# A gated-linear-attention stage in another order: TensorE turns tiles two ahead and across heads, GpSimd takes products and the normalising

## The reference

```python
log_a = log_sigmoid(lr @ w_a2 + b_a) / 16      # decay, 128 per head and token
b = cumsum(log_a)                              # within a chunk
q_t, k_t = q * 128 ** -0.5 * exp(b), k * exp(-b)
k_e = k * exp(b_last - b)
p = tril(q_t @ k_t.T)
o = p @ v + q_t @ S                            # S: state entering the chunk
S = exp(b_last) * S + k_e.T @ v
o = rmsnorm(o, g_head) * silu(g)               # then w_out
```

## Time and profile before

| | us |
|---|---|
| median of 3 runs | 3666.15 (3665.55 to 3667.69) |
| the profiled execution, its own time | 3667.28 |
| its span | 3665.7 |
| mean granted clock of TensorE | 0.953 |
| GLA, from the first state product (647.80) to the next stage's first load (1013.74) | 365.9 |

### The profile page before, as it was taken

One profiled execution on the slowest core, in us unless ns is written; L12 is line 12 of the kernel. 1 busy time (PEld: TensorE's weight loads), 2 busy tenths in 40 slices (PEclk: granted clock), 3 DMA queues, 4 the chain that ended last, 5 costly groups with the idle time before them and its releaser, 6 DMA issues. The chain is left out here.

```text
span 3665.7 us, 50108 instructions
## 1 busy us (share of the span) xinstructions
PE 3333.9 (91%) x17844; PEld 2414.2 (66%) x17844; DVE 1675.5 (46%) x2027; ACT 1398.8 (38%) x2277; POOL 718.8 (20%) x775
## 2 busy tenths in 40 slices
PE   7999997877779799999999799999999996888798
PEld 6999997433368699999999344444444443444387
DVE  5111121766633321111121589788888884333333
ACT  5111111545421111111111578777877783223321
POOL 0000000000001000000000466566666662000000
PEclk9999998888889899999999799999999998999899
DMA  4222122333254432222221623323232204999843
GB/s 140 70 69 69 64 65 77 110 115 117 77 185 165 142 116 69 69 71 74 74 64 54 179 80 95 90 64 93 81 109 53 58 18 138 368 365 372 324 146 105
DMA packets 240030, 439.34 MB, mean 120 GB/s; under 512 B 24821, under 2 KB 148538, under 8 KB 227802
## 3 DMA queue, kind: packets, MB, share of 16 engines
q1 hardware_dynamic: 224714, 351.87, 28.9%
q0 software_dynamic: 15152, 85.34, 6.5%
HBM read 313.03 MB, written 124.13 MB: 119 GB/s over the span
## 5 line engine op out<-in xcount | busy, mean ns | idle before, releaser
L1623 POOL TENSOR_TENSOR att_w<-att_w,att_rest 128x1023 f32<-128x1023 f32 (+7 forms) x384 | 613.1, 1599 | 375.5 <-DVE att_rest L1588 372.5
L451 PE MATMUL projb_acc<-projb_x_hi,projb_w_hi 128*128 128x416 f32 x1280 | 452.9, 354 | 26.5 <-DVE projb_x_lo L441 26.5
L451 PE MATMUL projb_acc<-projb_x_hi,projb_w_lo 128*128 128x416 f32 x1280 | 450.6, 352 | 0.0
L451 PE MATMUL projb_acc<-projb_x_lo,projb_w_hi 128*128 128x416 f32 x1280 | 450.3, 352 | 0.0
L1495 PE MATMUL att_z<-att_k,att_q 64*128 64x512 f32 (+3 forms) x1280 | 402.7, 588 | 2.7 <-ACT att_w L1546 2.7
L1538 ACT ACTIVATE att_rest<-att_z,att_bias 128x1024 f32<-128x1024 f32 (+7 forms) x384 | 332.8, 867 | 135.3 <-PE att_z L1495 113.7
L1459 PEld LDWEIGHTS att_wT_acc<-const_ident,att_w 128*128 128x128 f32 x2176 | 232.7, 141 | 216.5 <-issue 116.2
L1588 DVE TENSOR_TENSOR_SCAN att_rest<-att_rest,att_zero 128x128 f32<-128x128 f32 (+7 forms) x256 | 358.5, 1405 | 21.9 <-ACT att_rest L1538 21.1
L288 PE MATMUL proja_acc<-proja_x_hi,proja_w_hi 128*128 128x416 f32 x1000 | 353.5, 353 | 0.8 <-DVE proja_x_lo L261 0.7
L288 PE MATMUL proja_acc<-proja_x_hi,proja_w_lo 128*128 128x416 f32 x1000 | 351.4, 351 | 0.0
L288 PE MATMUL proja_acc<-proja_x_lo,proja_w_hi 128*128 128x416 f32 x1000 | 349.7, 350 | 0.0
(11 more groups left out here) (220 smaller groups left out, 4597.3 us busy)
## 6 DMA issues: line engine op xcount, KB each, us to landing
smp_k_pages<-in_cache_k SPq DMA_DIRECT2D x128, 512.0 KB, 9.2
smp_v_pages<-in_cache_v SPq DMA_DIRECT2D x128, 512.0 KB, 10.0
proj_b<-projb_out POOLq DMA_DIRECT2D x32, 1040.0 KB, 4.7
proj_a<-proja_out POOLq DMA_DIRECT2D x24, 1040.0 KB, 4.5
att_q<-proj_b SPq DMA_DIRECT2D x64, 256.0 KB, 4.0
att_k<-proj_b SPq DMA_DIRECT2D x14, 1024.0 KB, 12.8
proja_w_raw<-in_w_in_a SPq DMA_DIRECT2D x24, 512.0 KB, 4.1
gla_vgT<-proj_a SPq DMA_DIRECT2D x24, 512.0 KB, 6.1
```

The source lines that it names most:

```text
L451: mm = pe.matmul(acc[:, q, 0:size], w[:, b, k, :], x[:, k, at:at + size], start=(k == 0 and w is w_hi and x is x_hi), stop=(k == KD - 1 an ...
L1623: pool.tensor_tensor(these, these, passed[:, 1:size], ALU.mult).then_inc(w_made, 1)
```

## The change

`normalise_project` multiplies the gate by the head's gain `g_head` as well (`gate_gains`, one small load more), so that GLA needs no gain. In `gla`:

- TensorE turns tile t + 2 before it makes tile t's products across chunks and tile t + 1's products within. The list runs over the end of a head: tiles 0 and 1 of the next head are turned, and tile 0's inner products made, around the sample tile. Tile 0 has no product with a state, and the first chunk's state is copied, not cleared and updated; `S` is a ring of eight, and only the eighth chunk of a head waits until the old state is stored.
- GpSimd, which had nothing to do in GLA's loop, makes `gap`, the three products of a span, and the norm: one product with `rstd` broadcast over the span, one with the gate. It does so one span after the other, the last one of a head after the sample tile. The norm of span u is in the list at tile 4u + 5.
- The inverse root is exp(-0.5 ln(mean)) on ScalarE, in the table that exp and ln use already, and one Newton step of four small instructions on VectorE (`refine`). The factor 128 ** -0.5 goes into the exp as a bias.
- `logit`, `work`, `b_sum`, `gap` have two buffers; the steps are numbered 0 to 8.
- The eight sample state products use three buffers, and three of them come before the products with `s_in`.

The core of the diff:

```diff
+                    dve.scalar_tensor_tensor(out=out[:, b, at:at + size], in0=out[:, b, at:at + size],
+                                             scalar=gate_gains[:, b:b + 1], in1=acc[:, q, 0:size], op0=ALU.mult,
+                                             op1=ALU.mult).then_inc(gate_made, 1)
...
+        STEPS = (((7, 1), (8, 1)), ((0, 2), (1, 2), (2, 2), (3, 2)), ((4, 2),), ((5, 2), (6, 2)))
...
+        for t in range(NT):
+            order += [("turn", (t + 2) // n_tiles, (t + 2) % n_tiles), ("across", 0, t)]
+            order += [("root", 0, t // 4)] if t % 4 == 3 and t < NT - 1 else []
+            if t + 1 < NT:
+                order.append(("within", 0, t + 1))
+            order += [("normalise", 0, t // 4 - 1)] if t % 4 == 1 and t > 4 else []
+            for k, n in STEPS[t % 4]:
+                order.append(("prep", (t // 4 + n) // NCH, (t // 4 + n) % NCH, k))
+        order += [("sample", 0), ("root", 0, NCH - 1), ("turn", 1, 1), ("normalise", 0, NCH - 1), ("within", 1, 0)]
+        first = [("prep", 1, 0, k) for k in range(9)] + [("prep", 1, 1, k) for k in range(7)]
+        first += [("turn", 1, 0), ("turn", 1, 1), ("within", 1, 0)]
...
+                        pe.wait_ge(in_v[u], h * 16 + (16 * off + 16))
+                        pe.wait_ge(in_g[u], h * 16 + (16 * off + 16))
+                    pe.wait_ge(tok_cp, earlier + ONE)
...
+                    if t % 4 == 0 and t < NT:
+                        pe.wait_ge(keyed, h * (NCH * N_KEYED) + (off * NCH + u + 1) * N_KEYED)
...
+                def within(off, t):
+                    b, made = t % 2, h * n_tiles + (off * n_tiles + t + 1 + ONE)
+                    u, _ = place(t)
+                    pe.wait_ge(tok_cp, made)
+                    pe.wait_ge(ke_cp, made)
+                    pe.wait_ge(pt_cp, made)
+                    if t == 0 and h is not START:
+                        pe.wait_ge(s_smp, h * NSEQ + (NSEQ + ONE))
...
+                        if t >= 1:
+                            pe.wait_ge(s_made, h * NCK + (2 * t - 1 + half))
                         pe.matmul(ds_ps[:, half, 0:DV], ke[r, b, :], vg[r, u, t % 4, 0:DV], start=True,
                                   stop=True).then_inc(ds_mm, 1)
...
+                    if t >= 2:
+                        pe.wait_ge(o_cp, h * n_tiles + (t - 1))
+                    elif t == 0 and h is not START:
+                        pe.wait_ge(o_cp, h * n_tiles + n_tiles)
+                    pe.matmul(acc(t), pT[:, b, :], vg[:, u, t % 4, 0:DV], start=True, stop=True,
+                              skip_group_check=True)
+
+                def across(t):
+                    u, at = place(t)
                     for half in range(2):
...
+                        if ck == 0:
+                            continue
+                        pe.wait_ge(s_made, h * NCK + ck)
+                        r = slice(half * CHUNK, (half + 1) * CHUNK)
+                        mm = pe.matmul(o_ps[r, t % 2, 0:DV], qT[:, u, at + half * CHUNK:at + (half + 1) * CHUNK],
+                                       S[:, ck % 8, :], start=False, stop=True, skip_group_check=True)
...
+                    def new_state(q):
+                        if q < 3:
+                            pe.wait_ge(s_made, h * NCK + NCK)
...
+                            pe.wait_ge(s_smp, h * NSEQ + (q - 2 + ONE))
+                        pe.matmul(sample_ds(q), ke_smp[:, q, :], vg_smp[:, 0:DV], start=True, stop=True).then_inc(ds_smp, 1)
...
+            act.preload_act_table_set("natural_log_exp_and_others")
...
+                def inverse_root(u):
+
+                    act.wait_ge(sum_made, h * n_tiles + (end_of(u) + ONE))
+                    act.activation(log_mean[:, 4 * u:end_of(u)], sumsq[:, 4 * u:end_of(u)], ACT.Ln, scale=1.0 / DV,
+                                   bias=eps[:, :]).then_inc(log_made, 1)
+                    act.wait_ge(log_made, h * NCH + (u + 1))
+                    act.activation(rough[:, 4 * u:end_of(u)], log_mean[:, 4 * u:end_of(u)], ACT.Exp,
+                                   scale=-0.5).then_inc(rough_made, 1)
...
+                        elif k == 7:
+                            act.wait_ge(keyed, hk + (k0 + 1))
+                            act.activation(gap[:, e, 0:n], gap[:, e, 0:n], ACT.Exp, scale=1.0 / TAU).then_inc(expd, 1)
...
+                        if ck == 7:
+                            dve.wait_ge(state_stored, h * 16 + ONE)
+                        source = ds_ps[:, half, 0:DV]
+                        if ck == 0:
+                            dve.tensor_copy(S[:, 1, :], source).then_inc(s_made, 1)
+                            continue
+                        dve.wait_ge(s_made, h * NCK + (off * NCK + ck))
+                        dve.scalar_tensor_tensor(
+                            out=S[:, (ck + 1) % 8, :], in0=S[:, ck % 8, :], scalar=decay[:, t // 4, ck % 8:ck % 8 + 1],
...
+                def refine(u):
+
+                    cols, done = slice(4 * u, end_of(u)), h * (NCH * 4) + 4 * u
+                    dve.wait_ge(rough_made, h * NCH + (u + 1))
+                    dve.tensor_scalar(mean[:, cols], sumsq[:, cols], 1.0 / DV, EPS, ALU.mult, ALU.add).then_inc(refined, 1)
+                    dve.tensor_tensor(rstd[:, cols], rough[:, cols], rough[:, cols], ALU.mult).then_inc(refined, 1)
+                    dve.wait_ge(refined, done + 2)
+                    dve.scalar_tensor_tensor(out=mean[:, cols], in0=mean[:, cols], scalar=-0.5, in1=rstd[:, cols],
+                                             op0=ALU.mult, op1=ALU.mult).then_inc(refined, 1)
+                    dve.wait_ge(refined, done + 3)
+                    dve.scalar_tensor_tensor(out=rstd[:, cols], in0=mean[:, cols], scalar=1.5, in1=rough[:, cols],
+                                             op0=ALU.add, op1=ALU.mult).then_inc(refined, 1)
...
+                def normalise(u):
+                    pool.wait_ge(refined, h * (NCH * 4) + (4 * u + 4))
+                    pool.wait_ge(o_cp, h * n_tiles + end_of(u))
+                    scaled = pool.tensor_tensor(o[:, u, :, :], o[:, u, :, :], rstd[:, 4 * u:4 * u + 4].unsqueeze(2)
+                                                .broadcast_to([P, 4, DV]), ALU.mult)
+                    if u == NCH - 1:
+                        scaled = pool.tensor_tensor(o_smp[:, :], o_smp[:, :], rstd[0:SMP, NT:].broadcast_to([SMP, DV]),
+                                                    ALU.mult)
+                    scaled.then_inc(o_scaled, 1)
+                    pool.wait_ge(o_scaled, h * NCH + (u + 1))
+                    if u == NCH - 1:
+                        pool.tensor_tensor(o_smp[:, :], o_smp[:, :], vg_smp[:, DV:], ALU.mult)
+                    pool.tensor_tensor(o[:, u, :, :], o[:, u, :, :], vg[:, u, :, DV:], ALU.mult).then_inc(normed, 1)
...
+                            last = pool.tensor_tensor(gap[:, e, lo:lo + m * size].rearrange("p (c l) -> p c l", l=size),
+                                                      v[:, :, size - 1:size].broadcast_to([P, m, size]), v, ALU.subtract)
+                        last.then_inc(keyed, 1)
+                    else:
+                        pool.wait_ge(in_q[u], loads)
+                        pool.wait_ge(expd, he + (e0 + 3))
+                        pool.tensor_tensor(qT[:, u, 0:n], qT[:, u, 0:n], work[:, e, 0:n], ALU.mult).then_inc(keyed, 1)
+                        pool.wait_ge(in_k[u], loads)
+                        pool.tensor_tensor(ktT[:, u, 0:n], kT[:, u, 0:n], logit[:, e, 0:n], ALU.mult).then_inc(keyed, 1)
+                        pool.wait_ge(expd, he + (e0 + 4))
+                        pool.wait_ge(keyed, hk + (k0 + 3))
+                        pool.tensor_tensor(kT[:, u, 0:n], kT[:, u, 0:n], gap[:, e, 0:n], ALU.mult).then_inc(keyed, 1)
```

More of the change, by code:

```diff
@@ L17 @@
+import math
 from contextlib import ExitStack
@@ L504, in gla @@
         rT = s.sb("rT", [RANK, TOK])
-        logit, work, b_sum, gap = (s.sb(n, [P, wide]) for n in ("logit", "work", "b_sum", "gap"))
+        logit, work, b_sum, gap = (s.sb(n, [P, 2, wide]) for n in ("logit", "work", "b_sum", "gap"))
         keep = s.sb("keep", [P, wide])
@@ L761, in run @@
+                    pe.matmul(acc(NT), pT_smp[:, :], vg_smp[:, 0:DV], start=False, stop=True).then_inc(o_mm, 1)
+                    for q in range(3, NSEQ):
+                        new_state(q)
                 for kind, off, *x in items:
@@ L768, in run @@
                             for i, (at, n) in enumerate(parts):
[L769 removed]
+                                if h is not START or u or i:
+                                    pe.wait_ge(logit_cp, h * 5 + (place_of + i))
                                 pe.matmul(logit_ps[:, 0:n], w2[:, :], rT[:, at:at + n], start=True,
                                           stop=True).then_inc(logit_mm, 1)
[L772 to L781 removed]
+                    elif kind == "turn":
+                        to_tokens(off, *x)
+                    elif kind == "within":
```

(24 more changed lines are left out.)

438 lines of the change are left out of this document (165 added, 273 removed).

## The result

The changed kernel takes 3609.83 us (median of 4 runs, 3600.42 to 3621.19), the kernel before 3666.92 beside it; the ratio is 0.9845 (0.9816 to 0.9875). That is 57 us faster. The prediction was 3578 with a range of 3550 to 3608: right in direction, 32 us too low, and just outside its range. The changed kernel's own runs lie 21 us apart, the old one's 3.

The account below looks back on a forecast made before the run. GLA was taken as bound by waits between engines: 58.4 us per head plus late places 2.7, 2.4, 1.7, and 4% clock, gives 67.8; three plus 74.4 make 277.8, 88.1 less than 365.9, so 3578 us, range 3550 to 3608.

Parts of the forecast that it names:

- GLA 277.8: GLA's forecast length: three heads at 67.8 us and head 3 with its tail 74.4, instead of 365.9.
- the 76: Sign of being wrong: a head taking under 61 or over 76 us, where about 68 was expected.
- The tile with the root: Tiles 3, 7, 11: VectorE waits for the new root before updating states; 0.9 us each, 2.7 per head.
- the scan, which nobody needs for a tile: Tiles 3, 7, 11: the scan stands behind VectorE's root wait, claimed not needed for a tile; no term of its own.
- three places where the new order makes something late: Per head: root at tiles 3, 7, 11, 2.7 us; absolute value at 1, 5, 9, 13, 2.4; GpSimd at head's end, 1.7.
- GpSimd and VectorE get in each other's way: Rival: two-SBUF-input VectorE instructions wait for GpSimd's products; GLA gains about 73 us, total 3593, at worst 3608; chance 0.20.
- ScalarE waits for the absolute value, 0.6 each, 2.4 a head: Tiles 1, 5, 9, 13: ScalarE waits for it before copying the next turned tile; 0.6 us each, 2.4 per head.
- the clock: TensorE's granted clock in GLA taken as 0.95 from head 3's tiles; 4% added, giving 67.8 us per head.
- worth nothing by themselves: ScalarE's table loads in GLA, 9 per head at 1.28, 11.5 us: removal pays only by making results early.
- The wait moves: Rival: GpSimd's span 0 norm ends later, `w2` stays late behind `store_o(0)`; 8 us per head, 3602; chance 0.11.
- GpSimd becomes the bound: Rival: GpSimd's products take three times their rows, 110 us per head; GLA 455, total 3755; chance 0.03.
- The waits dissolve: Rival: the two-tile lead covers the three late places and TensorE keeps its clock; GLA 249, total 3550; chance 0.14.

Follow-up runs that it names:

- e_scan: Changed kernel with the scan alone one tile earlier on VectorE, behind the subtraction; the absolute value stays: 3587.9 us, ratio 0.9778.
- e_direct: Changed kernel with the decay as -ln(1 + exp(-z)), ScalarE's exponential reading PSUM, three VectorE instructions per span gone: 3589.8 us, ratio 0.9793.
- e_late: Changed kernel with a span's exponential and logarithm one tile later, behind the next tile's copy, and the subtraction later too: 3620.2 us, ratio 0.9875.
- e_nonorm: Changed kernel with GpSimd's two norm products cut to one column per tile, so prompt outputs are not normalised or gated: 3579.7 us, ratio 0.9768.
- e_abs2: Changed kernel with VectorE's absolute value taking one operand from PSUM instead of both from SBUF: 3598.9 us, ratio 0.9829.
- e_norm2: Changed kernel with the norm of span 2 behind tile 15's work in GpSimd's list, not tile 13's: 3601.7 us, ratio 0.9821.
- e_sqrt: Changed kernel with the inverse root back to a square root on ScalarE and a reciprocal on VectorE: 3640.1 us, ratio 0.9929.
- e_dscan2: Changed kernel with the direct logarithm, the scan one tile earlier and the norm of span 2 behind tile 15: 3560.8 us, ratio 0.9705.
- e_same: The changed kernel once more, unaltered, as the measure for the others: 3605.9 us, ratio 0.9843.
- e_best: Changed kernel with direct logarithm, scan one tile earlier, norm of span 2 behind tile 15 and a span's root one tile later: 3583.2 us, ratio 0.9776.

## Why the prediction was wrong, by its steps

**GLA 277.8, measured 308.3.** Heads 0 to 2, each to the next one's first state product, took 78.1, 77.5 and 75.1 us instead of 67.8; head 3 with its tail 77.6 instead of 74.4. The 30.5 us are spread over all heads, 10.3, 9.7, 7.3 and 3.2, the least in the last, which prepares no next head. 78 us in a head is past the 76 that the prediction itself had named as the sign of being wrong.

**Right, with their sizes.** A tile without a wait: 2.61 us (925.51 to 928.12), taken as 2.76 from the earlier trace rows. The table loads, the 10 us hole of the earlier trace rows and the waits of the earlier trace rows are gone. TensorE's wait for GpSimd's keys after a head's end: 2.1 us, taken as 1.7. The tile with the root: 2.99 us, 0.4 more than another, taken as 0.9 more. The tail from the sample output: 13.6 (944.39 to 957.99), taken as 14.9. The wait for `w2` doesn't show any more, taken as 1.0. GpSimd's products: 1.27 us for 512 columns (1.04 for `gap`), 1.89 for the one with `rstd` and 2.35 for the one with the gate, up to 2.69 where VectorE was first, taken as 1.18 and 2.2 from the earlier trace rows. Two slips of the sum move nothing: 12.8 less 11.2 is 1.6, not 1.7, and 242 us in GLA give 3542, not 3541.

**The step that failed first: "the scan, which nobody needs for a tile".** The prediction named three places where the new order makes something late, and this sentence took the scan out of them, so the sum has no term for it. But in tiles 3, 7, 11 and 15 the change's list has the scan directly ahead of ScalarE's exponentials, which wait for it, and the copy of the next turned tile stands behind them in ScalarE's queue. TensorE waited 20.1 us in 12 pieces that way. e_scan moves the scan by one tile, and the kernel is 18 us faster by the medians; beside e_direct the same move gives 24; e_late puts more ahead of it and costs 14.

**The second: GpSimd's norm was given its own length and nothing else.** e_nonorm puts it at 23 to 30 us beside the tail. The rival "GpSimd and VectorE get in each other's way", given 0.20 and 3593, is what the instructions show. The rule that I quoted there, of the Trainium skill's page "SBUF — State Buffer", section "Who interferes with whom", holds in this trace: with two SBUF inputs 692 ns became 1072 in the mean of those of 512 columns, and 2872 at most for 544; with one of them in PSUM it stayed at 751. The sum should have had a term by it. How much of the 23 to 30 us goes through this is open: 6.4 are the wait for GpSimd's keys at the heads' ends, 3.1 the shorter waits behind the absolute value, and most is TensorE's clock; the two kernels that take only a part of the contact away, e_abs2 and e_norm2, gain 7 and 4 us by the medians, neither clear of noise.

**Right in size, by luck: "ScalarE waits for the absolute value, 0.6 each, 2.4 a head".** TensorE's waits behind it are 10.0 us in 8 pieces, 2.5 a head. But the 0.6 took the absolute value at the 692 ns of the earlier trace rows, and a longer one met TensorE in 8 places where I had counted 14: without the norm, at 691 ns, it is 6.9 us. ScalarE's own 57.3 us in front of it are mostly time in which TensorE works.

**The third: the clock.** I took 4%, 0.95. The windows show 0.87 to 0.93. TensorE's busy time in GLA is 257.4 us at 0.89 and 237.0 at 0.96 for the same instructions: six tenths of what e_nonorm gave back. So the norm on GpSimd brings the clock down; by which path, and what decides when it falls, stays open. e_scan has 35.8 us of TensorE's idle time and a clock of 0.88, e_nonorm 38.1 and 0.96: the sum of idle time alone doesn't tell it.

**ScalarE's table loads "worth nothing by themselves".** I said that they pay only by making results early, and gave that no size. e_sqrt says 34 us for 47 of them: by the estimate above some 25 for the 35 that the change took out, near half of its gain.

**The other rivals.** "The wait moves" and "GpSimd becomes the bound" didn't happen: `w2` was in time, and GpSimd was busy for 38.8 of 77.6 us. "The waits dissolve" (3550, GLA 249) isn't the changed kernel, but e_dscan2 at 3561, GLA 262, shows that the tile list can nearly be brought there.

**What stays open.** Against e_same, by the medians: without the norm 26 us, with the scan earlier 18, with no absolute value 16, with the last two and the norm of span 2 moved 45. No kernel has the scan earlier and the norm out, so no single share can be given to each. And I didn't try the norm back on VectorE.

## What to carry to other kernels

When work goes to an idle engine, look at what its neighbour reads: GpSimd's product and a VectorE instruction with two SBUF operands ran one after the other here, even one of 4 columns. In an in-order queue, list what stands ahead of the instruction that the bounding engine waits for, tile by tile; a wait ahead of it counts as much as work, and a result that "nobody needs" yet can be what such a wait is for. Price a wait by what the bounding engine loses: ScalarE waited 57.3 us for the absolute value and 40.5 for the scan, TensorE lost 10.0 and 20.1 behind them. Moving one step by one tile gave a third of what the whole change had given.

## What the runs showed of the hardware that was not expected

- The hold is whole and goes both ways. VectorE's absolute value, begun 0.06 us after GpSimd's product, ended 0.58 us after that product's end (757.21 and 757.79); an instruction on 4 columns went from 0.16 to 1.24 us; and where VectorE was first, GpSimd's product took 3.21 us instead of 2.35.
- The product with the broadcast `rstd` (L989, 1.89 us for 1024 columns) holds VectorE as much as the one with two full operands (L998). An absolute value of 544 columns that overlapped L998 by 0.75 us, at 676.99, took 1.32 instead of 0.72: 0.60 lost. One of 512 that overlapped L989 by 0.80, at 693.28, took 1.35 instead of 0.69: 0.66 lost. L998 began beside the latter at 694.16 and took 2.69 instead of 2.35: VectorE was first.
- Two SBUF operands aren't the only case. In e_best VectorE's TENSOR_SCALAR of 4 columns with a single SBUF operand (L933) took 0.78 us at 731.99 beside GpSimd's product, and 0.17 in the changed kernel.
- The changed kernel's runs lie 21 us apart, those of the four kernels whose exponential doesn't wait for VectorE 3 to 8, those of the other changed ones 1 to 19. What sets it wasn't tried.
